# A two-layer mixer on one core: the first mixing stage takes its tiles from the fifth on, with its inputs issued in the stage before; in the attention POOL adds two halves ahead of the product with ones

## The reference, cut to what matters

```python
    y = jnp.concatenate([y_rwkv, y_attn], axis=-1) @ w_out      # first mixing, 1024 x 1024
    return x + y
...
        s = (jnp.einsum('bqhd,bkhd->bhqk', qn, k_nope)
             + jnp.einsum('bqhr,bkr->bhqk', qr, k_rope)).astype(jnp.float32) * scale
        p = jax.nn.softmax(s, axis=-1).astype(v.dtype)
        return jnp.einsum('bhqk,bkhd->bqhd', p, v)              # full attention, 12 heads
...
    return x + branch @ w_out                                   # second mixing
```

## Time and profile before

| | us |
|---|---|
| median of 3 runs (lowest, highest) | 4437.04 (4435.02, 4439.32) |
| profiled execution, its time | 4437.14 |
| its span in the profile | 4435.3 |
| TensorE busy | 3991.3 (90%) |
| DVE busy | 2721.7 (61%) |
| ACT busy | 2127.3 (48%) |
| POOL busy | 1148.1 (26%) |
| mean granted TensorE clock | 0.943 |

### The profile page before, as it was taken

How to read it: one execution, slowest core, us unless ns; L and a number is a source line. 1 busy time by engine, 2 the same in 40 slices (tenths; PEclk the granted TensorE clock), 3 DMA queues, 4 the chain that set the end, 5 groups by cost and what they waited for, 6 DMA issues and landing times. The chain is left out here.

```text
span 4435.3 us, 76406 instructions
## 1 busy us (share of the span) xinstructions
PE 3991.3 (90%) x31192; PEld 2801.1 (63%) x31192; DVE 2721.7 (61%) x5092; ACT 2127.3 (48%) x3127; POOL 1148.1 (26%) x918
## 2 busy tenths in 40 slices
PE   7989999778988888888679899798999999999989
PEld 5767767456656666666467687585555555555567
DVE  5556464556787788788565323244677777777443
ACT  4445454496778887687333222222333333333531
POOL 1111111126343343434111000000344444444200
PEclk9999999878999999999789999898999999999999
DMA  4333233311111112111166543555223232322233
GB/s 129 96 107 122 86 103 103 106 26 43 41 43 41 35 40 53 39 45 47 46 199 190 194 135 119 186 213 171 51 56 72 56 82 56 72 56 56 98 129 111
DMA packets 388094, 404.97 MB, mean 91 GB/s; under 512 B 115776, under 2 KB 287488, under 8 KB 387488
## 3 DMA queue, kind: packets, MB, share of 16 engines
q1 hardware_dynamic: 386224, 395.19, 30.7%
q10 hardware_dynamic: 1520, 4.89, 0.3%
HBM read 248.36 MB, written 151.62 MB: 90 GB/s over the span
## 5 line engine op out<-in xcount | busy, mean ns | idle before, releaser
L142 ACT ACTIVATE PT<-psum 128x1024 f32<-128x1024 f32 x384 | 394.4, 1027 | 695.0 <-PE psum L132 694.4
L170 DVE TENSOR_REDUCE m<-psum 128x1 f32<-128x1024 f32 x384 | 467.9, 1222 | 298.7 <-PE psum L132 298.7
L132 PE MATMUL psum<-xc,wah 128*128 128x512 f32 x1600 | 514.6, 403 | 3.2 <-DVE xc L146 2.9
L146 POOL TENSOR_TENSOR part<-PT 128x1024 f32<-128x1024 f32 x144 | 342.2, 2376 | 556.1 <-DVE all L146 381.3
L132 PE MATMUL psum<-PT,V 128*64 128x512 f32 x1536 | 370.3, 603 | 0.0
L143 ACT ACTIVATE bias<-score,cand,cols 128x2048 bf16<-128x2048 f32 (+6 forms) x217 | 314.4, 1449 | 102.9 <-DVE cand L158 95.7
L146 POOL TENSOR_TENSOR Lm<-gm,cst 64x512 f32<-64x512 f32 x192 | 258.9, 1348 | 383.2 <-PE psum L132 211.2
L132 PEld LDWEIGHTS psum<-xc,wah 128*128 128x128 f32 x1600 | 299.7, 190 | 79.4 <-issue 10.3
L143 ACT ACTIVATE sgn<-score,cand,cols 128x1920 bf16<-128x1920 f32 (+6 forms) x217 | 291.2, 1342 | 102.4 <-DVE cand L158 98.5
L132 PE MATMUL psum<-hc,w4h 128*128 128x512 f32 x1024 | 320.7, 395 | 11.4 <-ACT w4h L142 11.4
L132 PE MATMUL psum<-xc,wal 128*128 128x512 f32 x800 | 315.6, 395 | 0.0
(11 more groups left out here) (335 smaller groups left out, 8713.6 us busy)
## 6 DMA issues: line engine op xcount, KB each, us to landing
raw_a<-in_w_a SPq DMA_DIRECT2D x50, 512.0 KB, 3.9
raw_w<-in_w_in SPq DMA_DIRECT2D x32, 512.0 KB, 4.3
QNh<-scr_qnh SPq DMA_DIRECT2D x48, 256.0 KB, 4.9
QRh<-scr_qrh SPq DMA_DIRECT2D x96, 128.0 KB, 4.8
QNl<-scr_qnl SPq DMA_DIRECT2D x48, 256.0 KB, 6.7
xin<-in_x SPq DMA_DIRECT2D x16, 512.0 KB, 4.1
scr_AR<-AR SPq DMA_DIRECT2D x32, 256.0 KB, 2.2
scr_BK<-BK SPq DMA_DIRECT2D x32, 256.0 KB, 2.2
```

Of the source, the lines that this page charges most:

```text
L132: return self.e.matmul(out, a, b, start=start, stop=stop, skip_group_check=True)
L142: return self.e.activation(out, src, f, bias=bias, scale=scale)
L146: return self.e.tensor_tensor(out, a, b, op) if self.e else self.vector(out)
L170: return self.e.tensor_reduce(out, a, AX, op, negate=negate) if self.e else self.vector(a)
```

## The change

Four things. The sparse attention's SP list, at block 12 and block 14, gets loads of the first mixing stage: six weight chunks; x of its first tile and y of its first three. That stage keeps the loads of chunk 6 (SP) and 7 (ACT). Its tensors are laid out anew, so that these buffers lie where the blocks left over no longer need anything. It takes its tiles in the order 4 to 15, 0 to 3, and the projections take their chunks as 1, 2, 3, 0. In the attention POOL adds the two 512-column parts of each half in place (`half`, in step 2 of the next unit, behind DVE's last `acc`), TensorE multiplies only that with ones, and the `sum` stands behind the step's value products instead of ahead of them.

```diff
@@ sp_2, at ("pv", b, 0, 0)
                     q.dma(gate[:, :, :], feat("gaT")[:, :, 128 * nth(b):128 * nth(b) + 128]).then_inc(*d_gate.up(b))
+                    if nth(b) == 3:
+                        q.wait_ge(t_pe, "pv", b - 1, 3, last_of[b - 1])
+                        for c in range(6):
+                            q.dma(mix1.raw[c][:, :], mix1.weight[c]).then_inc(*mix1.d_w[c].up(c))
+                    if nth(b) == 1:
+                        q.wait_ge(k_act, "in", b - 2)
+                        q.wait_ge(k_act, "in", b - 1)
+                        q.wait_ge(d_yo, 6)
+                        q.dma(mix1.x[0][:, :], mix1.resid[mix1.rows_of(0), :]).then_inc(*mix1.d_r[0].up(0))
+                        for i in range(3):
+                            q.dma(mix1.y[i][:, :, :], feat("yT")[:, :, mix1.rows_of(i)]).then_inc(*mix1.d_y[i].up(i))
@@ class Mix
+            def rows_of(self, i):
+                n = (i + 4) % NT if self.top else i
+                return slice(128 * n, 128 * n + 128)
@@ mix_sp
-                    if c % 2 == 0 and M.top:
+                    if c == 6 and M.top:
                         q.dma(M.raw[c][:, :], M.weight[c]).then_inc(*M.d_w[c].up(c))
...
-                    if i < 3 and not M.top:
+                    if i < 3:
                         continue
                     q.wait_ge(M.dve, "yl", i - 3)
...
-                    if i == 0 and not M.top:
+                    if i == 0:
                         continue
@@ mix_act
-            for c in range(1, 8, 2) if M.top else ():
-                q.dma(M.raw[c][:, :], M.weight[c]).then_inc(*M.d_w[c].up(c))
+            if M.top:
+                q.dma(M.raw[7][:, :], M.weight[7]).then_inc(*M.d_w[7].up(7))
@@ projections
+        def chunk(c):
+            n = (c + 1) % 4
+            return slice(512 * n, 512 * n + 512)
@@ order_5
-            if r == 3 and u:
-                order_5.append(("sum", u - 1))
             many = 3 if u == 0 else 2
...
             if 1 < g < NST + 2:
                 order_5.append(("pv", g // 2 - 1, g % 2))
+            if u and r == 3:
+                order_5.append(("sum", u - 1))
             if u and r > 3:
                 order_5.append(("rc", u - 1, r - 4))
...
                 order_5.append(("acc", g - 2))
+            if u and r == 2:
+                order_5 += [("half", u - 1, 0), ("half", u - 1, 1)]
...
-        order_5 = order_5[:done] + order_m[:1] + end_5[:1] + order_m[1:3] + end_5[1:]
+        order_5 = order_5[:done] + order_m[:1] + end_5[:3] + order_m[1:3] + end_5[3:]
@@ pe_5
-                    q.wait_ge(q_dve, "acc", 8 * u + 7)
-                    for x in range(2):
-                        for w in range(2):
-                            t = q.mm(bank[6 + u % 2][64 * w:64 * w + 64, :], one[:, 0:64], all5[u % 2][w][:, x, :], x == 0, x == 1)
+                    q.wait_ge(q_pool, "half", u, 1)
+                    for w in range(2):
+                        t = q.mm(bank[6 + u % 2][64 * w:64 * w + 64, :], one[:, 0:64], all5[u % 2][w][:, 0, :])
@@ pool_5
+                elif k[0] == "half":
+                    u, w = k[1:]
+                    a = all5[u % 2][w]
+                    q.wait_ge(q_dve, "acc", 8 * u + 6 + w)
+                    q.tt(a[:, 0, :], a[:, 0, :], a[:, 1, :], ALU.add).then_inc(*q_pool.up("half", u, w))
```

More of the change, by code:

```diff
@@ L1803, in program @@
         P2.c.close()
+        PAD_V, PAD_S = 1480, 512
         class Mix:
@@ L1811, in __init__ @@
                 self.source, self.weight, self.resid, self.gain = source, weight, resid, gain
-                def rows():
-                    self.y = two(f"{name}_y", [128, 8, 128], n=3)
-                    self.x = two(f"{name}_r", [128, D], n=3)
+                if top:
+                    self.wh = sb(f"{name}_wh", [128, 8, D], FR)
+                    self.wl = sb(f"{name}_wl", [128, 8, D], FR)
+                    self.gf = sb(f"{name}_g", [128, D])
+                    self.junk = sb(f"{name}_j", [128, D], BF16)
+                    self.hjunk = sb(f"{name}_hj", [128, D], BF16)
+                    self.pad = [sb(f"{name}_pad0", [128, PAD_V])]
                     self.o = two(f"{name}_o", [128, D], n=3)
                     self.g = two(f"{name}_q", [128, D], n=3)
[L1817 to L1832, removed]
+                    later = two(f"{name}_r", [128, D])
+                    self.pad.append(sb(f"{name}_pad1", [128, PAD_S]))
+                    self.y = two(f"{name}_y", [128, 8, 128], n=3)
+                    self.x = [sb(f"{name}_r2", [128, D])] + later
+                    self.yh = two(f"{name}_yh", [128, 8, 128], FR)
+                    self.yl = two(f"{name}_yl", [128, 8, 128], FR)
                     self.hn = two(f"{name}_hn", [128, D])
-                    self.hjunk = sb(f"{name}_hj", [128, D], BF16)
                     self.hss = sb(f"{name}_hss", [128, 3 * NT])
@@ L1845, in __init__ @@
                     self.d_hh, self.d_hl = landings(name + "hh", 2), landings(name + "hl", 2)
+                else:
+                    self.y = two(f"{name}_y", [128, 8, 128], n=3)
+                    self.x = two(f"{name}_r", [128, D], n=3)
+                    self.o = two(f"{name}_o", [128, D], n=3)
+                    self.g = two(f"{name}_q", [128, D], n=3)
+                    self.gf = sb(f"{name}_g", [128, D])
+                    self.pad = sb(f"{name}_pad", [128, D])
+                    self.wh = sb(f"{name}_wh", [128, 8, D], FR)
+                    self.wl = sb(f"{name}_wl", [128, 8, D], FR)
+                    self.yh = two(f"{name}_yh", [128, 8, 128], FR)
+                    self.yl = two(f"{name}_yl", [128, 8, 128], FR)
+                    self.junk = sb(f"{name}_j", [128, D], BF16)
+                self.ss = sb(f"{name}_ss", [128, 3 * NT])
+                self.raw = self.o + self.g + self.x[1:3]
                 S.c.close()
@@ L1883, in mix_sp @@
                     i = k[1]
-                    if i < 3 and not M.top:
+                    if i < 3:
                         continue
                     q.wait_ge(M.dve, "yl", i - 3)
-                    q.dma(M.y[i % 3][:, :, :], feat(M.source)[:, :, 128 * i:128 * i + 128]).then_inc(*M.d_y[i % 3].up(i))
+                    q.dma(M.y[i % 3][:, :, :], feat(M.source)[:, :, M.rows_of(i)]).then_inc(*M.d_y[i % 3].up(i))
                 elif k[0] == "x":
                     i = k[1]
-                    if i == 0 and not M.top:
+                    if i == 0:
                         continue
@@ L1894, in mix_sp @@
                     q.wait_ge(M.dve, "o", i - 3, 1)
-                    q.dma(M.x[i % 3][:, :], M.resid[128 * i:128 * i + 128, :]).then_inc(*M.d_r[i % 3].up(i))
+                    q.dma(M.x[i % 3][:, :], M.resid[M.rows_of(i), :]).then_inc(*M.d_r[i % 3].up(i))
                 elif k[0] == "store":
@@ L1900, in mix_sp @@
                     q.wait_ge(M.d_o[i % 3], i - 3)
-                    q.dma(dst[128 * i:128 * i + 128, :], M.g[i % 3][:, :]).then_inc(*M.d_o[i % 3].up(i))
+                    q.dma(dst[M.rows_of(i), :], M.g[i % 3][:, :]).then_inc(*M.d_o[i % 3].up(i))
                 elif k[0] == "keep" and k[1] > 3:
                     i = k[1]
-                    sl = slice(128 * i, 128 * i + 128)
+                    sl = M.rows_of(i)
                     q.wait_ge(M.act, "hh", i, 1)
@@ L2090, in mix_pool @@
                          ALU.pow).then_inc(*M.pool.up("hrs", i))
-        retire()
         P4 = Stack()
         hc = [P4.sb("hc0", [128, 2, 8, 512], FR)]
+        mix1 = Mix("m1", "yT", A["w_out"], A["x"], A["final_g"], True)
+        retire()
         d_h = landings("h", 3)
-        mix1 = Mix("m1", "yT", A["w_out"], A["x"], A["final_g"], True)
         hc += [P4.sb(f"hc{i}", [128, 2, 8, 512], FR) for i in (1, 2)]
+        def chunk(c):
+            n = (c + 1) % 4
+            return slice(512 * n, 512 * n + 512)
         def load_h(q, c):
-            sl = slice(512 * c, 512 * c + 512)
+            sl = chunk(c)
             q.dma(hc[c % 3].bitcast(F32)[:, 0, :, :], feat("hTh")[:, :, sl]).then_inc(*d_h[c % 3].up(c, 0))
@@ L2724, in program @@
         end_5 = order_5[done:]
-        assert [k[0] for k in end_5] == ["sum"] + ["rc"] * 4 + ["out"]
-        order_5 = order_5[:done] + order_m[:1] + end_5[:1] + order_m[1:3] + end_5[1:]
+        assert [k[0] for k in end_5] == ["half"] * 2 + ["sum"] + ["rc"] * 4 + ["out"]
+        order_5 = order_5[:done] + order_m[:1] + end_5[:3] + order_m[1:3] + end_5[3:]
         order_5 += order_m[3:]
```

## The result

The changed kernel takes 4398.99 us (median of 4 runs, 4397.32 to 4403.22); the kernel before, run beside it, 4436.03 (4434.94 to 4439.32). The ratio is 0.9917 (95% interval 0.9901 to 0.9932), so 37 us or 0.8% faster. The forecast was 4392.6 with a range of 4386 to 4404: direction right and inside the range, 6.4 us too low, and 1 us outside the 4388 to 4398 that the prediction gave to its central case. The profiled execution has 4397.32 us, a span of 4395.4.

What follows compares the result with a forecast made beforehand. TensorE was taken as the bound, through a hole at the first mixing stage's start and its full queue in the attention. 4437.14 - 24.5 - 19.9 = 4392.7 us, the median 0.1 lower at 4392.6; range 4386 to 4404.

Steps and rivals of the forecast that it cites:

- central case: Both the early loads and the attention's sums work as worked out: 4388 to 4398 us, chance 0.80.
- The start, -24.5: First mixing stage: with inputs loaded early, chunk 7's product comes at 2227.2 instead of 2251.71, saving 24.5 us.
- 67 us to spare: First mixing stage's full part: DVE, busy 115 of 182 us, has room for the angle pass behind chunk 7.
- part one: First mixing stage starts with its inputs in place, by early loads of weights, x and y: -24.5 us.
- Blocks 12 to 15, 0: Sparse attention blocks given the early loads: SP has room, so no cost; bounds 0 to +3 us, taken as 0.
- From there the stage is full on TensorE with the same products in it: First mixing stage after chunk 7's product: same products, TensorE full, so the whole 24.5 us saved remains.
- Nothing for this: New tile and chunk order: same counts of instructions and loads, first four tiles still on chip, so 0 us.
- The attention, -20.4: Attention's full stretch: half the instructions with ones go, 0.885 us a unit in 23 units, 20.4 us saved.
- The rival in which POOL becomes the bound: Attention: every unit waits for POOL, slower than before from 2.6 us a half; 4455 us at 3.0; chance 0.03.
- The last unit, +0.45: Attention's last unit, without values to hide behind: one POOL add in between, sum 0.89 us shorter, net +0.45 us.
- halves late: Attention: POOL adds take 1.8 to 2.4 us, TensorE waits 0.2 to 1.4 a unit; 4397 to 4425 us; chance 0.06.
- start gains less: First mixing stage: late chunks, angle pass first or SP held up lose 2 to 8 us; 4395 to 4401; chance 0.09.

Runs made afterwards that it cites:

- phase_tail_again: Second run of the changed kernel with yh and yl moved 224 bytes on and the last unit's sum in four calls without POOL's halves: 4398.72 us, ratio 0.9903.
- pad32_before: The kernel before with 32 bytes of unused space ahead of the first mixing stage's yh and yl and 96 behind: 4442.32 us, ratio 1.0008.
- before128: The kernel before with 128 bytes of padding ahead of the first mixing stage's yh and yl: 4438.56 us, a single run.
- attn_only: The kernel before with only the attention's part of the change, the first mixing stage as it was: 4422.45 us, ratio 0.9963.
- half_twice: The changed kernel with each of POOL's halves done twice, once into a spare buffer: 4448.98 us, ratio 1.0017.
- sum_first: The changed kernel with TensorE's sum put back ahead of step 3's value products, POOL's halves kept: 4421.24 us, ratio 0.9957.
- after_again: The changed kernel, unaltered, run once more: 4404.53 us, ratio 0.9918.

## Why the prediction was right, and by what it was off

**The start, -24.5: -24.6.** The second mixing stage was a true template: 13.07 + 1.0 gave 14.07, the trace 14.06. The loads of chunks 6 and 7 were in time, and the angle pass went behind chunk 7. There it cost something: "67 us to spare" was right for the stage and wrong for its first turn. That turn waits for `m_hn`, DVE's, which ends a chain of small operations through POOL, and the wait is 0.89 us (1.60 in phase_tail_again, 0 before). It goes with part one: every run with the early loads has it, before, pad32_before, before128 and attn_only have none. That within part one the angle pass brought it is argued from its place and was not tested.

**Blocks 12 to 15, 0: +0.9**, inside its bounds and no more than the executions differ by: from block 12's gate load to the opening it is 88.9 to 91.1 us in the four profiles without early loads and 88.1 to 91.5 in the ten with them.

**The term that was missing.** "From there the stage is full on TensorE with the same products in it" is the step that failed, and with it the "Nothing for this" under the tiles' new order, since no term of the sum stood for the moved buffers: the products were the same, their pace was not. It was taken at 0 and measures 747 x 0.0060 = 4.5 us, with the wait 5.4 of the 5.5 in the account. The kernel's text showed it: buffers in another order and a padding of 1480 words. I read the padding as a matter of room only.

**The attention, -20.4: -19.2.** The count was right, 96 instructions for 192, and TensorE stayed full. The price of one was off: I took 1.77/8 = 0.221 us from the sum's own span, but that span ended at the next group's first instruction. Values and sum together shrink by 0.85, and the unit by 0.84; 23 x 0.84 = 19.3. POOL's half was 1.25 by forecast and 1.27 in the unit, slack 0.9 and 0.98, the wait without the new place 0.9 and 0.75. "The trace has none" was wrong of POOL's adds of 128x512: the second stage of the kernel before has rows of this very shape (groups of instructions by line and form), which say 1.29 without any scaling:

```profile
L146 POOL TENSOR_TENSOR yc<-yc,bo 128x512 f32<-128x512 f32 x16 | 20.6, 1288 | 1.3
```

The rival in which POOL becomes the bound had its turning point at 2.6 us for a half; at 2.55 half_twice is at 1.0017 of before. It was off by a little, since the turning point there counted part one's gain as 24.5 where it is 17 to 19.

**The last unit, +0.45: about +1.8 at the reciprocals.** The wait grew as forecast (1.38 to 2.72). What was left out is that the granted clock can stand at its lower level over the sum and behind it: of the 0.86 us that four instructions fewer save at full clock, 0.08 were left (1.78 for 1.86). At full clock the forecast held (0.49 in sum_first). DVE's small `mx` operation under POOL's half took 0.73 us instead of 0.17 and ended 0.02 after it. The Trainium skill (SBUF — State Buffer, SBUF: two separate sides) states an exclusive lock on the port pair that GpSimd shares with DVE, for a DVE operation with two SBUF inputs or in a 2-port mode; the row agrees, though it does not tell in which mode this one ran.

**The sum of it.** +5.5, +1.2 and +1.2 us (the last stage's 1.6 for 0.45) make 7.9. Against the kernel before beside it the change is worth 37.0 us, where 44.4 were forecast: 7.4. The time, 4399, lies among those of two rivals (halves late, start gains less), yet neither happened: no half is late in 23 units, and the start gained all it should. The range reached this far for those rivals' sake and not for a slower pace, so that it holds the measured time is in this part luck; that both parts gained, and by the mechanisms forecast, is not.

## What to carry to other kernels

Where the engine that bounds a stage does not wait, only its own instructions count, but their pace belongs to the count: when buffers move, compare the spacing of neighbouring products before and after, and keep an operand's address at the same rest by 256 as in the fast version (here 4.5 us). Work that is moved to a second engine is free only as long as it ends ahead of its consumer; look for a place in the bound engine's order that buys this time (here behind the values, worth 0.8 us a unit). A special case at the end of a loop has no such cover, and may be better left in the old form: here that put the reciprocals back at 5.58 us behind kmT.

## What the runs showed of the hardware

- Products of 128x512 in fp32r follow each other at 0.2271 to 0.2273 us or at 0.2323 to 0.2333, at a granted clock of 1.00, by the start address of the operand that is loaded as weights: fast at a rest of 128 by 256, slow at rests of 0 and 160. The operand that streams through was at a rest of 128 each time.
- A POOL add of two 128x512 fp32 operands in SBUF takes 1.26 to 1.30 us, of 128x1024 2.38; DVE's of 128x512 takes 0.68.
- Behind waits of 2.72 and 3.38 us for the last unit's sum TensorE's granted clock mostly showed its lower level (0.55 in the window of the changed kernel, from 0.7 us into the sum on in after_again), but behind the same 2.72 us in sum_first it was 1.00 over the sum; behind the 1.38 us of the kernel before the sum's eight instructions ran at full pace.
